# Eight token buffers and GpSimd norm weights in the prologue of a decoder layer, with gate rows and the first head's loads moved a block up

## The reference, cut to what matters

```python
def rms_norm(x, w):
    y = x * lax.rsqrt(jnp.mean(x * x, axis=-1, keepdims=True) + EPS)
    return y * w

xn = rms_norm(h, norm_mix_w[l])
proj = jnp.einsum('bsd,de->bse', xn, w_in[l])      # 8 heads x (q k v | ml_q ml_k ml_v ml_o), gates
# differential attention on q, k, v; chunkwise mLSTM on ml_*, with per-head rows made of ml_i, ml_f
h = h + merged @ w_out
h = h + relu(rms_norm(h, norm_ffn_w) @ w_ff1)**2 @ w_ff2
return rms_norm(h, final_norm_w)
```

## Time and profile before

| what | us |
|---|---|
| runs (median of 3) | 2007.83 |
| lowest, highest | 2005.05, 2009.06 |
| the profiled execution, its own time | 2009.17 |
| span of its trace | 2007.4 |
| PE busy | 1923.8 |
| DVE, ACT, POOL busy | 1180.8, 966.1, 364.8 |

### The profile page before, as it was taken

One profiled execution on the slowest core, in us unless ns is written; L12 is line 12 of the kernel. 1 busy time (PEld: TensorE's weight loads), 2 busy tenths in 40 slices (PEclk: granted clock), 3 DMA queues, 4 the chain that ended last, 5 costly groups with the idle time before them and its releaser, 6 DMA issues. The chain is left out here.

```text
span 2007.4 us, 26057 instructions
## 1 busy us (share of the span) xinstructions
PE 1923.8 (96%) x9378; PEld 1605.9 (80%) x9378; DVE 1180.8 (59%) x1537; ACT 966.1 (48%) x1634; POOL 364.8 (18%) x204
## 2 busy tenths in 40 slices
PE   5989999999999999999998999999999999999998
PEld 4768888788888787878886888888888888888886
DVE  5736666566575757543321112278677787888874
ACT  4346565556465555544433333225765765533341
POOL 1211211212111121211121444441000000021002
PEclk9989999999999999999999999999999999999999
DMA  5562657645544546273435443645686785563422
GB/s 150 88 153 66 148 84 131 99 120 107 123 104 110 120 72 158 59 176 70 68 88 162 155 150 104 224 157 210 220 289 210 255 281 196 210 237 132 163 82 84
DMA packets 207825, 291.79 MB, mean 145 GB/s; under 512 B 36840, under 2 KB 127592, under 8 KB 200832
## 3 DMA queue, kind: packets, MB, share of 16 engines
q1 hardware_dynamic: 195520, 281.98, 50.9%
q10 hardware_dynamic: 12224, 8.72, 1.3%
HBM read 203.56 MB, written 87.10 MB: 145 GB/s over the span
## 5 line engine op out<-in xcount | busy, mean ns | idle before, releaser
L716 PE MATMUL gp<-r1h,w_hi 128*128 128x512 f32 x1152 | 457.4, 397 | 13.9 <-ACT ev L1062 12.3
L718 PE MATMUL gp<-r1h,w_lo 128*128 128x512 f32 x1152 | 452.1, 392 | 0.0
L717 PE MATMUL gp<-r1l,w_hi 128*128 128x512 f32 x1152 | 451.6, 392 | 0.0
L1967 POOL TENSOR_TENSOR w_lo<-w_raw,w_hi 128x1024 fp32r<-128x1024 f32 x88 | 219.2, 2491 | 896.8 <-ACT w_hi L1057 896.8
L716 PEld LDWEIGHTS gp<-r1h,w_hi 128*128 128x128 f32 x1152 | 218.2, 189 | 59.7 <-issue 8.1
L718 PEld LDWEIGHTS gp<-r1h,w_lo 128*128 128x128 f32 x1152 | 217.8, 189 | 46.6
L717 PEld LDWEIGHTS gp<-r1l,w_hi 128*128 128x128 f32 x1152 | 218.3, 189 | 42.3
L977 PE MATMUL scores<-xh,qh 128*128 128x512 f32 x512 | 200.1, 391 | 1.4 <-ACT res L1367 1.3
L981 PE MATMUL scores<-xh,ql 128*128 128x512 f32 x512 | 199.3, 389 | 0.0
L979 PE MATMUL scores<-xl,qh 128*128 128x512 f32 x512 | 199.2, 389 | 0.0
L1207 ACT ACTIVATE pr<-scores,nb 128x256 f32<-128x256 f32 (+7 forms) x128 | 93.9, 739 | 122.2 <-DVE nb L1601 120.6
(11 more groups left out here) (340 smaller groups left out, 3650.8 us busy)
## 6 DMA issues: line engine op xcount, KB each, us to landing
xraw<-xo_d SPq DMA_DIRECT2D x54, 1024.0 KB, 5.1
proj_d<-ev SPq DMA_DIRECT2D x128, 256.0 KB, 3.2
rq<-in_w_ff SPq DMA_DIRECT2D x32, 1024.0 KB, 7.8
w_raw<-in_w_in SPq DMA_DIRECT2D x56, 512.0 KB, 9.2
xo_d<-res SPq DMA_DIRECT2D x78, 256.0 KB, 3.2
xo_d<-ring SPq DMA_DIRECT2D x60, 256.0 KB, 2.9
pr<-proj_d SPq DMA_DIRECT2D x16, 512.0 KB, 5.6
gt<-proj_d SPq DMA_DIRECT2D x32, 256.0 KB, 2.7
```

The source lines that it names most:

```text
L716: pe.matmul(gp[half][:], wh[slot][:, k, :], mh[:, k, t], start=(k == 0), stop=False)
L717: pe.matmul(gp[half][:], wh[slot][:, k, :], ml[:, k, t], start=False, stop=False)
L718: mm = pe.matmul(gp[half][:], wl[slot][:, k, :], mh[:, k, t], start=False, stop=(k == KT - 1))
L1967: pool.tensor_tensor(wl[slot][:], raw[slot][:], wh[slot][:].bitcast(F32), ALU.subtract).then_inc(w_split, 1)
```

## The change

XB becomes 8: each token tile has its own buffer, and SP no longer waits between x loads. The weights of the norm are multiplied on GpSimd (`x_weight`), in place, after the square of the tile has been taken; DVE then multiplies by the reciprocal alone. The low part of weight block 0 moves from GpSimd to DVE. Five constant loads move from ACT's queue to SP's, behind x tile 7 and before weight block 1; ACT's first activation and its load of `wif` now wait for GpSimd's two memsets. ACT makes the high part of block 0 at t == 4 and not at 6. In round 0 PE turns `yrow` at k == 6 and not 7 and makes the small product at k == 8 and not 9; ACT's steps 8, 9, 10 become 7, 8, 9. SP stores the two rows in round 0, b == 5, and issues `att_loads(0)` in round 1 before the weights of block 8. Some semaphores are merged, with counts changed to match.

```diff
-XB = 4
+XB = 8
@@ SP
-                    sp.wait_ge(init_done, 3)
+                    sp.wait_ge(init_done, 5)
@@
-                wait(sp, x_tr, 2 * (j - XB + 1))
                 sp.dma_start(xtok[j % XB][:], x2[j * P:(j + 1) * P, :]).then_inc(x_in[j % XB], 16)
@@
-                if j == 4:
-                    sp.dma_start(cosT[:].bitcast(I32), positions[0].partition_broadcast(P)).then_inc(c2_in, 16)
-                    sp.dma_start(inv[:], c_inv).then_inc(c2_in, 16)
-                    sp.dma_start(sg[:, 0:3 * P], c_mask).then_inc(c2_in, 16)
-                    sp.dma_start(keep[:], c_keep).then_inc(c2_in, 16)
-                if j == 6:
-                    wload_head(0, 1)
+            sp.dma_start(gb[0:NH, :], ...).then_inc(c_in, 16)
+            sp.dma_start(gb[32:32 + NH, :], ...).then_inc(c_in, 16)
+            sp.dma_start(lamt[:], ...).then_inc(c_in, 16)
+            sp.dma_start(carry[:], c_carry).then_inc(c_in, 16)
+            sp.dma_start(last[:], c_last).then_inc(c_in, 16)
+            wload_head(0, 1)
+            sp.dma_start(cosT[:].bitcast(I32), positions[0].partition_broadcast(P)).then_inc(c2_in, 16)
+            sp.dma_start(inv[:], c_inv).then_inc(c2_in, 16)
+            sp.dma_start(sg[:, 0:3 * P], c_mask).then_inc(c2_in, 16)
+            sp.dma_start(keep[:], c_keep).then_inc(c2_in, 16)
             wload_head(0, 2)
@@ head_round of SP
+                    if first and b == 5:
+                        sp.wait_ge(pro_dve, 4)
+                        sp.dma_start(u_d, urow[:]).then_inc(uw_st, 16)
+                        sp.wait_ge(pro_act, 3)
+                        sp.dma_start(inter_d, wrow[:]).then_inc(uw_st, 16)
+                    if second and b == 0:
+                        att_loads(att)
                     if b + 2 < HB:
...
-                    if isinstance(h, int) and h == 1 and b == 0:
-                        sp.wait_ge(pro_dve, 4)
-                        sp.dma_start(u_d, urow[:]).then_inc(uw_st, 16)
-                        sp.wait_ge(pro_act, 3)
-                        sp.dma_start(inter_d, wrow[:]).then_inc(uw_st, 16)
...
-                        if b == 0:
+                        if b == 0 and not second:
                             att_loads(att)
@@ PE
-                if k == 7:
+                if k == 6:
                     pe.wait_ge(pro_dve, 4)
...
-                if k == 9:
+                if k == 8:
                     pe.wait_ge(pro_act, 4)
@@ ACT
-            act.wait_ge(init_done, 1)
+            act.wait_ge(init_done, 3)
             act.activation(rstd0[:, 0:1], ones[:, 0:1], ACT.Sqrt)
...
-            act.dma_start(gb[0:NH, :], ...).then_inc(c_in, 16)
-            act.dma_start(gb[32:32 + NH, :], ...).then_inc(c_in, 16)
-            act.dma_start(lamt[:], ...).then_inc(c_in, 16)
-            act.dma_start(carry[:], c_carry, ...).then_inc(c_in, 16)
-            act.dma_start(last[:], c_last, ...).then_inc(c_in, 16)
...
-                if t == 6:
+                if t == 4:
                     split_hi(0, 0, 0)
@@ DVE
-                    xt = xtok[(t - 1) % XB]
-                    dve.scalar_tensor_tensor(xt[:], xt[:], r, nwb[:], ALU.mult, ALU.mult).then_inc(x_scaled, 1)
+                    dve.wait_ge(x_weighted, t)
+                    dve.tensor_scalar(xtok[t - 1][:], xtok[t - 1][:], r, None, ALU.mult).then_inc(x_scaled, 1)
...
+                if t == 5:
+                    dve.wait_ge(w_hi, 1)
+                    dve.tensor_tensor(wl[0][:], raw[0][:], wh[0][:].bitcast(F32), ALU.subtract).then_inc(w_split, 1)
@@ GpSimd
+            def x_weight(t):
+                if t == 0:
+                    pool.wait_ge(nwb_in, 16)
+                pool.wait_ge(ss_ready, t + 1)
+                pool.tensor_tensor(xtok[t][:], xtok[t][:], nwb[:], ALU.mult).then_inc(x_weighted, 1)
+            for t in range(4):
+                x_weight(t)
             pool.wait_ge(wif_h, 2)
...
-            split_lo(0, 0)
+            for t in range(4, TT):
+                x_weight(t)
```

More of the change, by code:

```diff
@@ L326, in build @@
         ss_ready, x_var, x_std, x_rstd, x_scaled = (sem(n) for n in ("ss_ready", "x_var", "x_std", "x_rstd", "x_scaled"))
-        x_tr, x_hi, x_lo = sem("x_transposed"), sem("x_hi"), sem("x_lo")
-        x_out, x_col = sem("x_turned_out"), [sem("x_column6_in"), sem("x_column7_in")]
-        sq_ready, sq_used, std_ready = sem("sq_ready"), sem("sq_used"), sem("std_ready")
+        x_tr, x_out, x_lo = sem("x_transposed"), sem("x_turned_out"), sem("x_lo")
+        sq_ready, sq_used = sem("sq_ready"), sem("sq_used")
         s_ready, d_ready = sem("s_ready"), sem("d_ready")
         ss_done = sem("sumsq_done")
-        wif_set, wif_h, wif_l = sem("wif_set"), sem("wif_h"), sem("wif_l")
+        x_weighted, wif_h, wif_l = sem("x_weighted"), sem("wif_h"), sem("wif_l")
         pdv, pact = sem("prologue_dve"), sem("prologue_act")
@@ L365, in build @@
         ft_tr, ft_out, out_st = sem("ft_tr"), sem("ft_out"), [sem("out_st0"), sem("out_st1")]
-        xcol_in = stg_in + x_in + x_col
         DVE_HEAD = 46
@@ L469, in _, with head_round @@
                     wload_head(0, 0)
-                if j == 4:
-                    sp.dma_start(cosT[:].bitcast(I32), positions[0].partition_broadcast(P)).then_inc(c2_in, 16)
-                    sp.dma_start(inv[:], c_inv).then_inc(c2_in, 16)
-                    sp.dma_start(sg[:, 0:3 * P], c_mask).then_inc(c2_in, 16)
-                    sp.dma_start(keep[:], c_keep).then_inc(c2_in, 16)
-                if j == 6:
-                    wload_head(0, 1)
+            sp.dma_start(gb[0:NH, :], ml_gate_b[0, 0:NH].rearrange("(p a) -> p a", a=1)).then_inc(c_in, 16)
+            sp.dma_start(gb[32:32 + NH, :], ml_gate_b[0, NH:2 * NH].rearrange("(p a) -> p a", a=1)).then_inc(c_in, 16)
+            sp.dma_start(lamt[:], da_lambda[0].rearrange("a b -> (a b)").partition_broadcast(P)).then_inc(c_in, 16)
+            sp.dma_start(carry[:], c_carry).then_inc(c_in, 16)
[5 more added lines that the diff above has]
+            sp.dma_start(keep[:], c_keep).then_inc(c2_in, 16)
             wload_head(0, 2)
-            def head_round(h, att, first=False, last=False):
+            def head_round(h, att, first=False, second=False, last=False):
                 for b in range(HB):
@@ L510, in _ @@
             head_round(0, None, first=True)
-            head_round(1, 0)
+            head_round(1, 0, second=True)
             with sp.Fori(2, NH - 1) as h:
@@ L545, in x_column @@
                 sp.dma_start(xcol[i][:].rearrange("p (t n) -> p t n", t=TT),
-                             x2.rearrange("(t p) n -> p t n", p=P)[:, :, k * P:(k + 1) * P]).then_inc(xcol_in[i], 16)
+                             x2.rearrange("(t p) n -> p t n", p=P)[:, :, k * P:(k + 1) * P]).then_inc(x_in[i], 16)
             for j in range(2 * KT):
@@ L773, in attend @@
                     pe.wait_ge(pro_act, 7)
-                    pe.wait_ge(init_done, 3)
+                    pe.wait_ge(init_done, 5)
                 if s in (0, 2):
@@ L940, in wo_step @@
                         pe.wait_ge(obt, 2 * NH)
-                    wait(pe, x_out, 2 * (i - 1) + half + 1 if i else 0)
-                    pe.wait_ge(xcol_in[i], 16 * (KT + 1 if i < 2 else TT // XB + 1 if i < 2 + XB else 1))
+                    pe.wait_ge(x_out, 2 * TT + (2 * (i - 1) + half + 1 if i else 0))
+                    pe.wait_ge(x_in[i], 32)
                     for j in range(4):
@@ L1089, in _ @@
                         act.activation(r1h[:, 4 * i:4 * i + 4, (t - 2) * P:(t - 1) * P],
-                                       (tr, ob)[i][:].rearrange("p (k n) -> p k n", k=4), ACT.Copy).then_inc(x_hi, 1)
+                                       (tr, ob)[i][:].rearrange("p (k n) -> p k n", k=4), ACT.Copy).then_inc(x_out, 1)
                 if t == 3:
                     act.wait_ge(wif_in, 16)
-                    act.wait_ge(wif_set, 2)
+                    act.wait_ge(init_done, 3)
                     act.activation(wifh[:, :, 0:NH], wif[:, :, 0:NH], ACT.Copy).then_inc(wif_h, 1)
                     act.activation(wifh[:, :, 32:32 + NH], wif[:, :, NH:2 * NH], ACT.Copy).then_inc(wif_h, 1)
-                if t == 6:
+                if t == 4:
                     split_hi(0, 0, 0)
@@ L1123, in prologue_step @@
                     act.activation(wrow[:], yrow[32:32 + NH, :], ACT.Exp).then_inc(pro_act, 1)
-                if k == 8:
+                if k == 7:
                     act.wait_ge(pro_pe, 3)
@@ L1135, in prologue_step @@
                         act.activation(tab[:], tab[:], ACT.Sin).then_inc(pro_act, 1)
-                if k == 10:
+                if k == 9:
                     act.wait_ge(pro_pe, 4)
@@ L1321, in q_hi_part, with x_out_part @@
                 act.activation(qh[s % 3][:], quarter_of(s)[:], ACT.Copy).then_inc(p_hi, 1)
-            def x_hi_part(s):
+            def x_out_part(s):
                 if s == 0:
@@ L1354, in _ @@
                     q_hi_part(0)
```

(18 more changed lines are left out.)

4 lines of the change are left out of this document (1 added, 3 removed).

## The result

The first comparison, four runs each: 1992.82 us median (1991.52 to 1994.42) against 2006.44 (2003.76 to 2009.06), ratio 0.9935, 95% interval 0.9921 to 0.9949.

The account below looks back on a forecast made before the run. The prediction took PE's stream, busy 1923.8 of 2007.4 us, as the bound, so edits count only by moving PE's stops. Loads -11.1 and tiles +2.6 gave -8.5, from median 2007.8 to 1999.3 us; range 1994.0 to 2006.0.

Parts of the forecast that it names:

- The tiles: Prologue up to `gates_half(0)`: its start moves from 28.32 to near 30.95, +2.6 us.
- The block: Tile loop: DVE's scaling stands until GpSimd's multiplication on SBUF operands has finished, ending 0.54 us behind it.
- I take 10.0: Prologue: token tile 1 lands at 10.0 us, where it was 11.98 before.
- the long issue lies beside `lamt`'s: Prologue: SP's 2.65 us issue of tile 1 coincides with ACT's queue issuing `lamt`, taken as reason for the earlier landing.
- The walk: Prologue: tile-by-tile times for ACT, GpSimd, DVE and PE, from tile 1 landed at 10.0 to gates near 30.95.
- From there PE has the same work: From `gates_half(0)` on: PE's work is unchanged, with tiles 5, 6, 7 ready before their places.
- The loads of the first head: Slot 0 of round 1: earlier loads remove PE's stop for `pr`, -9.4 us, -11.1 with the slow stretch behind it.
- So another -1.7 us: Behind the `pr` stop: PE's slow stretch of eight transposes and four matmuls goes too, -1.7 us.
- rival 1: Prologue: the ports don't bite, sum -14.6, 1993.2; or the block with tile 1 at 7.5, -11.0, 1996.8; together 0.15.
- Rival 2: Round 1: `pr` stays late, holding 5 to 9.4 us of the stop; sum about -4 to +1; chance 0.16.
- Rival 3: Prologue: tile 1 lands no sooner, 11.4 to 12.0; sum -7.1 to -6.5, 2001.0; chance 0.20.
- Rival 4: Prologue: GpSimd becomes the bound, with tiles 5 to 7 in the chain; +5.9, 2013.7; chance 0.06.

Follow-up runs that it names:

- e2: The changed kernel with only the moved row stores, first-head loads and PE and ACT steps undone: 2005.83 us, 0.9998 of before.
- e8: The changed kernel with ACT's load of `wif` sent ahead of its wait for GpSimd's memsets, constants still on SP: 1994.88 us, 0.9943 of before.
- e3: The kernel before, unchanged, run as a second program: 2008.47 us, 1.0003 of before.
- e1: The kernel before with only the moved row stores, first-head loads and PE and ACT steps: 1996.03 us, 0.9949 of before.
- e5: The changed kernel, unchanged, run again beside the runs of before (the second comparison): 1993.33 us, 0.9939 of before.
- e10: The kernel before with one added wait, so ACT sends `wif` and the constants only behind GpSimd's two memsets: 2003.08 us, 0.9984 of before.
- e9: The changed kernel with the scaling by the reciprocal done by ACT and not DVE, GpSimd's weights kept: 1991.02 us, 0.9925 of before.
- e7: The changed kernel with norm weights back on DVE and each tile's root, reciprocal and scaling behind its own square: 1986.80 us, 0.9907 of before.

## Why the prediction was wrong where it was

**The tiles: this is the step that failed.** The prediction put them at +2.6 us; the traces show +0.1 in the first pair and +0.4 in the mean of three traces on each side, and `e2` measured 0.9998 (0.9987 to 1.0009). The block itself was right: DVE's scaling took 2.3 to 2.65 us where it met GpSimd, and ended 0.54 to 0.56 behind it; the pace was 3.4 to 4.0 us a tile. What was wrong around it:

- "I take 10.0", the landing of token tile 1: it was squared at 8.7, which takes 1.3 off the 2.6. Its reason failed too, "the long issue lies beside `lamt`'s": `e8` shows that it was `wif`'s load.
- The walk itself was 0.5 us too long, 29.12 against 30.95 - 1.3. That leaves +0.8 at `gates_half(0)`, against the 28.32 of before.
- "From there PE has the same work": it has, but not the same time. PE is slow at the start of the gates, for a stretch that differs between executions, and from `gates_half(0)` to `gates_half(1)` takes 16.6 to 17.8 us over all traces. It took 17.5 in the first trace of before and 16.7 in `e3` and `e1`; 16.9 in after, 16.8 in `e2` and 17.3 in `e5`. One trace could not carry a term of 1 us here, and 0.7 of the 0.8 us was gone at `gates_half(1)`.

**The loads of the first head: right.** `kraw` was expected at 104.7 and came at 104.97, `dc` near 104.6 and came there, `pr` at 108.3 or later and came at 108.78; the stop went whole, nothing behind it became late. The stop with its slow stretch cost 11.0 us in the trace that the prediction read, as its -11.1 says. "So another -1.7 us" is still a size read from one execution: four slow matmuls there, nine, eight and three in `e3`, `e2` and `e10`, so that the slow stretch cost 1.5 to 2.7 us, and the whole 11.75 in the mean of four. Loads alone measure 10.2 us (7.2 to 13.0 by the interval).

**The sum.** -11.75 and +0.4 in place of -11.1 and +2.6 give -11.4. The second comparison measured -12.2 (-9.4 to -15.2), the first -13.6 (-10.2 to -15.9); both intervals hold -11.4. What is left, 0.8 and 2.2 us, fits the scatter behind slot 2, but isn't shown to be that. Of the 6.5 us by which the time missed 1999.3, 1.4 are the reference: the forecast started from the median of three runs of before, 2007.83, and with the fourth it is 2006.44. From 2006.44 the mended sum gives 1995.1, inside the range; that both medians, 1992.82 and 1993.33, lie about 1 us below its end of 1994.0 is this open rest. By its own text the range left out rival 1's low part with 0.04. The first measured change lies between rival 1's two forms, -11.0 and -14.6, but not because the ports don't bite: every scaling that met GpSimd stood behind it.

**The rivals.** Rival 1 fell in its first form and came half true in its second, the block with an early tile: tile 1 at 8.7 and not 7.5. Rival 2 fell: no DMA wait at slot 0 in any trace with the moved loads. Rival 3 fell, and with it the 0.6 us that I had estimated for the moved constants as the whole gain of the landing: tile 1 came 3.2 us sooner. Rival 4 fell: tiles 5 to 7 were ready in time, with no wait of PE between 29.12 and 45.97.

The Trainium skill (SBUF — State Buffer, "SBUF: two separate sides") says that DVE and GpSimd hold a shared port pair for a whole instruction, and that a DVE instruction contends when it runs in a two-port mode, or when it has two SBUF inputs and GpSimd's instruction reads SBUF. The traces agree: TENSOR_SCALAR stood behind GpSimd as above; so did the two-input low part of block 0 (2.18 us at 28.98, beside GpSimd's 27.69 to 30.08). In `e9` the same instruction of DVE began first, at 27.26, and took 1.22; there GpSimd's instruction of 27.62 took 3.08 and not 2.35. The low parts of the tiles, with one operand in PSUM, kept 0.68 us at 27.79 and 28.39 in the changed kernel, inside GpSimd's 27.69 to 30.08.

## What to carry to other kernels

Before work goes from DVE to GpSimd, ask whether the two then run at the same moment on SBUF operands: 1.28 us on DVE became 2.3 to 2.65 us of standing, and the tile loop ended 4.5 us sooner with the work back on DVE. At the start of a kernel, look at what is issued beside the large loads that the first work waits for: holding back one load of 64 KB in 1024 pieces by one wait gave 3.2 us. And price a stretch in which PE is slow from several traces: behind the same stop it cost 1.5 to 2.7 us, and at the start of the gates it hid 0.7 us of a forecast term.

## What the runs showed of the hardware that was not expected

A load of 64 KB in 1024 pieces, sent by ACT at 0.75 us, stretched SP's next three issues from 1.40 to 4.23 us, for a reason that stays open; sent at 2.62 it did not, and the 512 KB tile behind it landed 2.3 us sooner. At the very start PE ran matmuls at a pitch of 0.43 us, as behind the `pr` stop where the granted clock is under 1, but the windows there (22 to 27 us in `e7`) record a granted clock of 1.00; why the record doesn't show it stays open. The same wait of 1.9 us is followed by a lower granted clock in one execution and not in another, and the clock lost this way ranged from 8.5 to 13.7 us in thirteen traces of nearly the same stream.
